# Unscaled first blocks at three norms, a norm of the input by chunks, and modulation blocks summed earlier

## The chip, the cores and the metric

The kernel runs on one core of one Trainium2 chip. The metric is the device time of one launch in microseconds (us). Three runs of the kernel before took 2051.9, 2055.06 and 2056.86 us; the median is 2055.06 us.

## The reference

Two transformer blocks are applied to a sequence of 512 tokens of 1024 features, all in float32. Cut to the parts that matter here:

```
mod = silu(c) @ w_mod[l] + b_mod[l]          # 6 vectors of 1024 for each of 2 layers
sh1, sc1, g1, sh2, sc2, g2 = split(mod, 6)
u  = rms_norm(h,  norm1_g) * (1 + sc1) + sh1      # layer 0: tokens x
uc = rms_norm(ctx, norm1_g) * (1 + csc1) + csh1   # layer 0: 256 context tokens, own c_ctx
f, q, k, v = split(u @ w_in); kc, vc = split(uc @ w_in[:, 1024:])
q, k, kc = rms_norm over each head of 64
y = concat(fourier_mix(f), neighbourhood_attention(q, k, v, kc, vc)) @ w_out
h = h + g1 * y
h = h + g2 * (relu(modulate(rms_norm(h, norm2_g), sh2, sc2) @ w1) ** 2) @ w2
# layer 1: the same with a pooling mixer in place of the attention
# second block:
h = h + merged(rmsnorm(h, norm_mix_g) @ w_in_2 ...) @ w_out_2
u = rmsnorm(h, norm_ffn_g)
h = h + (silu(u @ w_gate) * (u @ w_up)) @ w_down
return rmsnorm(h, norm_final_g)
```

A root-mean-square norm divides each token by one number and multiplies each feature by a gain. So `(g * h / r) @ w` equals `((g * h) @ w) / r`: the division by `r`, one number for each token, may stand behind the product. A shift `s` that is added before the product adds `s @ w`, one number for each output feature.

## The kernel before, in words

All activations lie transposed in SBUF: 8 chunks (KC) of 128 features by 512 tokens. `h` is the residual. A product takes its input as a high and a low part, `uh`/`ul` or `ah`/`al`. Its weights come in blocks of 1024 by 256 (1 MB). SyncE (SP) loads block b into one of four `raw` buffers, ScalarE (ACT) rounds it to `wh` (`split`, L495), GpSimd (POOL) subtracts to get `wl` in four instructions (L880), and TensorE (PE) runs three passes for each chunk and each half of the block (L982 to L984): 48 matmuls of 512 columns. There are two buffers of `wh`/`wl` and four PSUM banks for products, two to a block, so block b needs the buffers and the banks of block b-2 back. Nothing but this fixed order and the semaphores sets the schedule: each engine has its program written out by hand, and every semaphore wait stands in that program.

**Norms** (`norm_sum`, L1028 on; `norm`, L1460 on). ACT squares the chunks of `h`, POOL adds them up, PE sums over the partitions with matmuls of one column (L1041, L1044), ACT takes the root (L511), DVE the reciprocal (L1457), PE spreads it over the partitions (L1050), and DVE and ACT build chunk by chunk: DVE scales (L1467), ACT rounds (`highs`, L523 or L525), DVE subtracts (L1474 or L1472). Small matmuls (`keep_clock`, L1026) are put between. The products behind the norm begin as chunks arrive. The names of the norms are x and ctx (opening), mlp0, pool, mlp1, mix2, ffn and final.

**Opening.** The vectors sh1 and sc1 for x and for ctx come from 8 weight blocks `modf`. PE multiplies them by the two columns of `csil` as stationary operand (L1072), giving 2 rows by 2048; DVE copies the rows, and PE turns them into columns (L1077). Then the norm of x is built, then blocks 0 and 1 (v, by token), the norm of ctx, and the context's v (from L982 with `uch`). Blocks 2 to 7 (k, q, f) follow; beside them run ten head norms (`HN`): PE sums (L1084), ACT root (L551 or L553), DVE reciprocal and product (L1533, L1536), in the places that `HN_AFTER` lists. Block 4 needs the banks that head norms 0 and 1 free.

**Modulation.** The other modulation vectors come from 40 blocks `w_modr`, in the order m = 0, 1, 2, ... DVE sums a block in four instructions (`mod_sum`, L1498 and L1501), PE turns two blocks' sum into columns (`mod_columns`, L1061: four fp32 matmuls of one column, shown as eight instructions), DVE stores them (`mod_store`, L1511). Blocks 0 to 3 stand in the opening, 4 to 11 (`MOD_EARLY` to `MOD_MID`) in the Fourier stage, 12 to 15 beside w_out, 16 on in the first MLP. SP loads block m after block m-2 is summed, in its one queue, in program order with the weights and with 32 small copies `vwin`.

## Time and profile before

| | before |
|---|---|
| median of 3 runs | 2055.06 us |
| profiled execution, its own time | 2056.09 us |
| span of the profile | 2054.2 us |
| PE busy (matmul) | 2002.2 us, 97% |
| DVE, ACT, POOL busy | 930.8, 667.1, 920.0 us |
| mean granted TensorE clock | 0.987 of full |

The profiled execution's own time is 1.9 us above its span; the span is what the engines' rows cover. PE busy is the share of time with a matmul in flight, not the share of peak.

### The profile page before, as it was taken

What the parts mean: (1) busy time and instruction counts of PE and PEld (TensorE: products, weight loads), DVE (VectorE), ACT (ScalarE), POOL (GpSimd) and SP (SyncE); (2) the same over time, 40 slices, a digit from 0 to 9 for tenths busy, and PEclk for the clock granted to TensorE, in tenths of its full rate; (3) what the DMA queues carried; (4) which work ended last, traced back from release to release, by engine and by line L of the source; (5) the groups of instructions that cost most, each with busy time, mean ns of one, the idle gap of its engine ahead of it and who ended that gap; (6) DMA issues with size and microseconds to landing.
All of it is one profiled execution on the core that took longest, in us unless ns stands there. A gap on an engine that the chain in (4) does not pass through costs nothing. (4 is left out here: it accounts for less than half of the span.)

```text
span 2054.2 us, 25743 instructions
## 1 busy us (share of the span) xinstructions
PE 2002.2 (97%) x10096; PEld 1633.8 (80%) x10096; DVE 930.8 (45%) x1422; ACT 667.1 (32%) x872; POOL 920.0 (45%) x704
## 2 busy tenths in 40 slices
PE   7998899999999999999999999999999999999998
PEld 3886578888888888888888866888888878888887
DVE  0546885755748352323233265266664433223123
ACT  2322553222212332212223355356554232222122
POOL 2333345545555535445445312543444455444445
PEclk9899999999999989999999999999999999999999
DMA  8144341625334222222222202222222222222221
GB/s 350 57 143 150 131 152 75 246 91 194 147 153 175 84 83 92 102 102 83 101 102 89 82 22 78 82 83 83 72 73 82 103 82 89 96 102 100 85 82 42
DMA packets 42629, 222.92 MB, mean 109 GB/s; under 512 B 12721, under 2 KB 13233, under 8 KB 17329
## 3 DMA queue, kind: packets, MB, share of 16 engines
q1 hardware_dynamic: 42544, 221.77, 30.0%
q8 instruction: 57, 0.93, 0.2%
q14 instruction: 28, 0.22, 0.0%
HBM read 217.55 MB, written 2.10 MB: 107 GB/s over the span
## 5 line engine op out<-in xcount | busy, mean ns | idle before, releaser
L880 POOL TENSOR_TENSOR wl<-raw,wh 128x512 fp32r<-128x512 f32 x611 | 836.4, 1400 | 1010.9 <-ACT wh L495 911.7
L982 PE MATMUL bank<-uh,wh 128*128 128x512 f32 x1480 | 590.8, 399 | 2.2 <-DVE ul L1472 0.5
L984 PE MATMUL bank<-uh,wl 128*128 128x512 f32 x1480 | 576.9, 390 | 0.0
L983 PE MATMUL bank<-ul,wh 128*128 128x512 f32 x1480 | 576.7, 390 | 0.0
L495 ACT ACTIVATE wh<-raw 128x2048 fp32r<-128x2048 f32 (+1 forms) x149 | 281.3, 1888 | 589.6 <-PE bank L984 586.8
L982 PEld LDWEIGHTS bank<-uh,wh 128*128 128x128 f32 x1480 | 277.8, 188 | 76.8 <-issue 11.1
L984 PEld LDWEIGHTS bank<-uh,wl 128*128 128x128 f32 x1480 | 277.8, 188 | 59.2
L983 PEld LDWEIGHTS bank<-ul,wh 128*128 128x128 f32 x1480 | 278.0, 188 | 58.1 <-issue 3.6
L982 PE MATMUL bank<-ah,wh 128*128 128x512 f32 x816 | 321.3, 394 | 0.0
L984 PE MATMUL bank<-ah,wl 128*128 128x512 f32 x816 | 320.3, 393 | 0.0
L983 PE MATMUL bank<-al,wh 128*128 128x512 f32 x816 | 317.5, 389 | 0.0
L984 PEld LDWEIGHTS bank<-ah,wl 128*128 128x128 f32 x816 | 153.2, 188 | 34.7
L983 PEld LDWEIGHTS bank<-al,wh 128*128 128x128 f32 x816 | 153.2, 188 | 34.3
L982 PEld LDWEIGHTS bank<-ah,wh 128*128 128x128 f32 x816 | 153.4, 188 | 31.3 <-issue 0.2
L1611 DVE SCALAR_TENSOR_TENSOR h<-bank,modc,h 128x512 f32<-128x512 f32 x72 | 53.3, 750 | 268.1 <-PE bank L984 268.1
L1501 DVE SCALAR_TENSOR_TENSOR acc<-mraw,csil,acc 128x512 f32<-128x512 f32 x112 | 141.0, 1259 | 3.7
L638 ACT ACTIVATE r<-bank 128x512 f32<-128x512 f32 x64 | 38.3, 598 | 249.4 <-PE bank L984 248.8
L1641 DVE TENSOR_TENSOR v<-r 128x512 f32<-128x512 f32 x64 | 51.6, 807 | 115.7 <-ACT r L638 115.7
L982 PE MATMUL bank<-wh,uh 128*128 128x256 f32 (+1 forms) x256 | 76.3, 298 | 8.9 <-DVE ul L1474 7.3
L1609 DVE TENSOR_TENSOR h<-bank,h 128x512 f32<-128x512 f32 x32 | 22.1, 692 | 136.7 <-PE bank L984 136.7
L983 PE MATMUL bank<-wl,uh 128*128 128x256 f32 (+1 forms) x256 | 74.1, 290 | 0.0
L984 PE MATMUL bank<-wh,ul 128*128 128x256 f32 (+1 forms) x256 | 74.0, 289 | 0.0
(228 smaller groups left out, 1982.5 us busy)
## 6 DMA issues: line engine op xcount, KB each, us to landing
raw<-in_w SPq DMA_DIRECT2D x64, 1024.0 KB, 5.5
mraw<-in_w_modr SPq DMA_DIRECT2D x32, 1024.0 KB, 4.9
raw<-in_w_gu SPq DMA_DIRECT2D x22, 1024.0 KB, 4.9
raw<-in_w_hg SPq DMA_DIRECT2D x16, 1024.0 KB, 5.0
modf<-in_w_modf SPq DMA_DIRECT2D x8, 1024.0 KB, 17.9
raw<-in_w_in SPq DMA_DIRECT2D x8, 1024.0 KB, 16.7
raw<-in_w_out SPq DMA_DIRECT2D x8, 1024.0 KB, 6.0
mmid<-in_w_modr SPq DMA_DIRECT2D x8, 1024.0 KB, 4.9
```

The costliest lines, as they stand in the source:

```text
L495: act.activation(wh[:, b % 2, 0:nk], raw[:, s, 0:nk], ACT.Copy).then_inc(split_hi, 1)
L638: act.activation(r1[:, m % 2], bank[bi][:], ACT.Relu).then_inc(bank_free[bi], 1)
L880: last = pool.tensor_tensor(wl[:, b % 2, k:k + 2], raw[:, b % RAW, k:k + 2], f32(wh[:, b % 2, k:k + 2]), ALU.subtract)
L982: pe.matmul(out, ah_, bh, start=first, stop=False)
L983: pe.matmul(out, ah_, bl, start=False, stop=False)
L984: return pe.matmul(out, al_, bh, start=False, stop=last)
L1501: dve.scalar_tensor_tensor(a, part[:, k], csil[:, k0 + k, 0:1], a, ALU.mult, ALU.add).then_inc(macc, 1)
L1609: ins = dve.tensor_tensor(h[:, m, :], bank[bi][:], h[:, m, :], ALU.add)
L1611: ins = dve.scalar_tensor_tensor(h[:, m, :], bank[bi][:], gate, h[:, m, :], ALU.mult, ALU.add)
L1641: dve.tensor_tensor(v1[:, m % 2], r1[:, m % 2], r1[:, m % 2], ALU.mult).then_inc(square_ready, 1)
```

## The change

1. *Opening by chunks.* The `modf` blocks are reordered so that block u holds shift and scale of chunk u. `csil` is padded to 32 columns (`csilp`), and the 8 chunks of a block go to four groups of 32 output partitions (`first_rows`). ACT copies 128 by 256, and two matmuls with `sel` add the four partial sums into columns (`first_columns`). DVE makes the gain (`columns_ready`), scales, and subtracts for this chunk, and PE multiplies blocks 0 and 1 by that chunk (`chunk_products`). x is loaded in two halves ahead of the `modf` blocks, its squares are added by DVE, those of ctx by POOL. 30 `keep_clock` matmuls begin the program.
2. *Unscaled first blocks.* At mlp0, mix2 and ffn (`EARLY`) ACT and DVE also make a high and low part of `h` times the gain, without the division (`plain_highs`, `plain_lows`). The first block takes these (`first_product`), with the norm's sum put before its chunk 2 and the spread before its chunk 4. DVE copies the spread factors (`rsb`) and, when the norm is done, multiplies the first block's two banks by them into `tt` (`first_scale`); ACT goes on from `tt`. For mlp0 the shift's part is 16 fp32 matmuls of one column on the raw weights (`shift_columns`), added as a bias.
3. *Modulation.* `MOD_EARLY` goes from 4 to 8: blocks 4 to 7 are summed before the first head norm.
4. The ffn's loop of two and the first group of mlp0 are written out.

```diff
-MOD_EARLY, MOD_MID = 4, 12
+EARLY = {"mlp0": 0, "mix2": 1, "ffn": 2}
+MOD_EARLY, MOD_MID = 8, 12
 # SP, opening
-            sp.dma_start(modf[:, 0], t["w_modf"][0]).then_inc(modf_in[0], 16)
-            sp.dma_start(h[:], t["xT"]).then_inc(x_in, 16)
-            for i in range(1, 8):
-                if i == 6:
-                    load(0, t["w_in"][0])
+            for i in range(2):
+                sp.dma_start(h[:, 4 * i:4 * i + 4, :], t["xT"][:, 4 * i:4 * i + 4, :]).then_inc(x_in[i], 16)
+            load(0, t["w_in"][0])
+            for i in range(8):
                 sp.dma_start(modf[:, i], t["w_modf"][i]).then_inc(modf_in[i], 16)
+                if i == 3:
+                    load(1, t["w_in"][1])
+                if i == 5:
+                    sp.dma_start(ctxT[:], t["ctxT"]).then_inc(ctx_in, 16)
...
             for b in range(8):
                 if 4 <= b + 2 <= 8:
                     load(b + 2, t["w_in"][b + 2] if b < 6 else t["w_out"][0])
-                if b < MOD_EARLY:
-                    load_mod(b)
+                if 2 * b < MOD_EARLY:
+                    load_mod(2 * b)
+                    load_mod(2 * b + 1)
 # ACT
-            squares("mlp0", h, (6, 7))
+            statistics("mlp0", (6,))
+            split(FIRST["mlp0"] + 1)
+            statistics("mlp0", (7,))
             root("mlp0")
-            highs("mlp0", lambda k: mod(0, 3, k), uh, beside=FIRST["mlp0"] + 1)
+            highs("mlp0", lambda k: mod(0, 3, k), uh)
...
+                            if first and j == 0:
+                                act.wait_ge(bank_free[bi], used(b0) + 1)
+                                act.wait_ge(ccol_ready, 1)
+                                act.wait_ge(square_ready, SQ0 + 32 * layer + m - 1)
+                                act.activation(r1[:, m % 2], tt[:, half], ACT.Relu, bias=ccol[:, half:half + 1]).then_inc(first_done, 1)
+                                continue
 # PE
+            def first_product(name, b):
+                def ready(k):
+                    if k == 2:
+                        norm_sum(name)
+                    if k == 4:
+                        norm_spread(name)
+                    pe.wait_ge(xlo_ready, 8 * EARLY[name] + k + 1)
+                product(b, *plain(name), ready=ready)
+            def first_rows(u):
+                pe.wait_ge(modf_in[u], 16)
+                if u >= 2:
+                    pe.wait_ge(mod0_ready, u - 1)
+                for k in range(KC):
+                    g = k % 4
+                    last = pe.matmul(bank[4 + u % 2][32 * g:32 * g + 32, 0:2 * P], csilp[:, k, :], modf[:, u, k, :], start=(k < 4), stop=(k >= 4))
+                last.then_inc(rows_full, 1)
+            for u in (2, 3, 4):
+                first_rows(u)
+                chunk_products(0, u - 2)
+                first_columns(u)
+            chunk_products(0, 3)
+            first_rows(5)
+            first_columns(5)
+            chunk_products(0, 4)
+            first_rows(6)
+            chunk_products(0, 5)
+            first_columns(6)
...
+            MOD_AT = {(2, 0): 1, (3, -1): 2, (4, 0): 3}
...
-                mod_columns(MOD_EARLY // 2 + g)
+                if g < 2:
+                    mod_columns(MOD_EARLY // 2 + g)
+            def shift_columns(b):
+                pe.wait_ge(raw_full[b % RAW], 16 * (b // RAW + 1))
+                for half in range(2):
+                    for k in range(KC):
+                        last = pe.matmul(bank[4][:, half:half + 1], raw[:, b % RAW, k, P * half:P * half + P], mod(0, 3, k), start=(k == 0), stop=(k == KC - 1))
+                last.then_inc(ccol_full, 1)
 # DVE
+                if name == "x":
+                    for k in range(KC):
+                        scaled(k)
+                        low(k)
+                        if k < KC - 1:
+                            columns_ready(k + 1)
+                    return
...
+            def first_scale(name, b):
+                for half in range(2):
+                    bi = bank_of(b, half)
+                    dve.wait_ge(bank_full[bi], used(b) + 1)
+                    if half == 0:
+                        dve.wait_ge(rsb_ready, EARLY[name] + 1)
+                        dve.wait_ge(ulo_ready, 8 * NORM[name] + 8)
+                    dve.tensor_tensor(tt[:, half], bank[bi][:], rsb[:], ALU.mult).then_inc(bank_free[bi], 1)
```

The change moves instructions at three places that matter below. The first is PE at the start of the program, before the change; `modf`/`csil` are the modulation rows, `con` is the identity or the ones, `wh`/`uh` the first product.

```order
L1072 MATMUL bank<-modf,csil 2x256 x32
L1041 MATMUL bank<-con,sqs_94 128x1 x4
L1044 MATMUL bank<-con,sq 128x1 x4
L1050 MATMUL bank<-con,rc 128x128 x4
L1072 MATMUL bank<-modf,csil 2x256 x32
L1077 MATMUL bank<-con,modrow 128x2 x16
L982 MATMUL bank<-wh,uh 128x256
```

The same engine and place after the change.

```order
L1121 MATMUL bank<-con 128x128 x30
L1185 MATMUL bank<-con,sqx 128x1 x4
L1201 MATMUL bank<-modf,csilp 32x256 x8
L1147 MATMUL bank<-con,rc 128x128 x4
L1208 MATMUL bank<-con,modrow 128x2 x2
L1201 MATMUL bank<-modf,csilp 32x256 x8
L1208 MATMUL bank<-con,modrow 128x2 x2
L1201 MATMUL bank<-modf,csilp 32x256 x8
L1221 MATMUL bank<-wh,uh 128x256
```

The first product begins after three of eight row groups instead of after all of them. The second place is DVE between the norm of ctx and the first head norms, before; `acc` is a modulation sum, `RECIPROCAL tt` the start of a head norm.

```order
L1498 TENSOR_SCALAR acc<-mraw,csil 128x512
L1501 SCALAR_TENSOR_TENSOR acc<-mraw,csil,acc 128x512 x7
L1511 TENSOR_TENSOR modc<-bank,bmod 128x4
L1498 TENSOR_SCALAR acc<-mraw,csil 128x512
L1501 SCALAR_TENSOR_TENSOR acc<-mraw,csil,acc 128x512 x3
L1533 RECIPROCAL tt<-tt 128x512
L1536 SCALAR_TENSOR_TENSOR kT<-bank,vec,tt 128x512
```

After:

```order
L1727 TENSOR_SCALAR acc<-mraw,csil 128x512
L1730 SCALAR_TENSOR_TENSOR acc<-mraw,csil,acc 128x512 x7
L1727 TENSOR_SCALAR acc<-mraw,csil 128x512
L1730 SCALAR_TENSOR_TENSOR acc<-mraw,csil,acc 128x512 x7
L1740 TENSOR_TENSOR modc<-bank,bmod 128x4
L1727 TENSOR_SCALAR acc<-mraw,csil 128x512
L1730 SCALAR_TENSOR_TENSOR acc<-mraw,csil,acc 128x512 x7
L1740 TENSOR_TENSOR modc<-bank,bmod 128x4
L1727 TENSOR_SCALAR acc<-mraw,csil 128x512
L1730 SCALAR_TENSOR_TENSOR acc<-mraw,csil,acc 128x512 x7
L1740 TENSOR_TENSOR modc<-bank,bmod 128x4
L1762 RECIPROCAL tt<-tt 128x512
```

Twelve instructions on three blocks have become 32 on eight, all ahead of the first head norm. The third place is ACT around the norm mlp0, before; `uh<-tt` are the high parts behind the norm, `wh<-raw` a weight split (L493 and L484 are the halves of block 13), `r` the ReLU of a finished block.

```order
L506 ACTIVATE sq<-h 128x512 [waits sq_added,bank_free3]
L511 ACT_TABLE_LOAD
L511 ACTIVATE rc<-bank,con 128x4 [waits sum_full]
L525 ACTIVATE uh<-tt,modc 128x512 [waits t_ready] x2
L493 ACTIVATE wh<-raw 128x1024 [waits bank_full3,raw_full1]
L525 ACTIVATE uh<-tt,modc 128x512 [waits t_ready]
L484 ACTIVATE wh<-raw 128x1024
L525 ACTIVATE uh<-tt,modc 128x512 [waits t_ready] x5
```

After:

```order
L529 ACTIVATE wh<-raw 128x2048 [waits bank_full3,raw_full1]
L540 ACTIVATE sq<-h 128x512 [waits sq_added,bank_free3]
L548 ACTIVATE ah<-h,gm 128x512 [waits bank_free3]
L560 ACT_TABLE_LOAD
L560 ACTIVATE rc<-bank,con 128x4 [waits sum_full]
L574 ACTIVATE uh<-tt,modc 128x512 [waits t_ready] x8
L711 ACTIVATE r_107<-tt,ccol 128x512 [waits square_ready,ccol_ready,bank_free0]
L711 ACTIVATE r_107<-tt,ccol 128x512 [waits square_ready,ccol_ready,bank_free1]
L529 ACTIVATE wh<-raw 128x2048 [waits bank_full1,raw_full2]
```

The split of block 13 has moved ahead of the last square. The split of block 14 (the last row) stands behind two ReLUs that read `tt`, which DVE writes after the whole norm; they used to read the banks of block 12 (`r<-bank`).

## Rows read from the trace of the kernel before

**Rows 1.** Who PE waited for: total us, times, longest us.
```profile
PE bank L1061 <- DVE modc L1511: 5.6, 2, 3.5
PE bank L1061 <- DVE acc L1501: 4.8, 1, 4.8
```
**Rows 2.** Timeline of PE, opening: start us, us, line, out<-in, count [idle before].
```profile
9.85 6.39 PE L1072 MATMUL bank<-modf,csil 128*2 128x256 f32 x16 [9.85 <-DMA modf<-in_w_modf]
17.12 10.52 PE L1072 MATMUL bank<-modf,csil 128*2 128x256 f32 x48 [0.88 <-DMA modf<-in_w_modf]
...
45.15 3.73 PE L1077 MATMUL bank<-con,modrow 2*128 2x2 f32 x32
...
86.41 0.28 PE L982 MATMUL bank<-wh,uch 128*128 128x256 f32 x1
...
134.83 0.80 PE L982 MATMUL bank<-uh,wh 128*128 128x512 f32 x1
```
**Rows 3.** Timeline of ACT and DVE, opening.
```profile
29.71 1.90 ACT L495 ACTIVATE wh<-raw 128x2048 fp32r<-128x2048 f32 x1
...
51.14 0.75 DVE L1474 SCALAR_TENSOR_TENSOR ul<-tt,modc,uh 128x512 fp32r<-128x512 f32 x1
...
75.11 0.87 DVE L1467 SCALAR_TENSOR_TENSOR tt<-ctxT,gm,bank 128x256 f32<-128x256 f32 x2 [0.80 <-PE bank L1050]
...
82.31 0.48 DVE L1474 SCALAR_TENSOR_TENSOR ucl<-tt,modx,uch 128x256 fp32r<-128x256 f32 x1 [0.18 <-ACT uch L525]
```
**Rows 4.** Timeline of DVE and SP, 82 to 127 us.
```profile
83.23 5.54 DVE L1501 SCALAR_TENSOR_TENSOR acc<-mraw,csil,acc 128x512 f32<-128x512 f32 x7
...
99.67 4.16 DVE L1501 SCALAR_TENSOR_TENSOR acc<-mraw,csil,acc 128x512 f32<-128x512 f32 x3
...
123.50 3.35 DVE L1533 RECIPROCAL tt<-tt 128x512 f32<-128x512 f32 x1 [19.68 <-ACT tt L553]
...
95.81 20.98 SPq L405 DMA_DIRECT2D vwin<-vnat  x32
```
**Rows 5.** DMA issues of the page: count, KB each, median us to landing.
```profile
mraw<-in_w_modr SPq DMA_DIRECT2D x32, 1024.0 KB, 4.9
```
**Rows 6.** Timeline of PE at the norms mlp0, mix2 and ffn.
```profile
327.00 0.95 PE L1061 MATMUL bank<-con,acc 128*128 128x1 f32 x8
...
358.61 1.05 PE L1061 MATMUL bank<-con,acc 128*128 128x1 f32 x8
...
1097.46 0.40 PE L984 MATMUL bank<-ah,wl 128*128 128x512 f32 x1
...
1128.59 0.39 PE L982 MATMUL bank<-uh,wh 128*128 128x512 f32 x1
...
1672.65 0.39 PE L984 MATMUL bank<-uh,wl 128*128 128x512 f32 x1
...
1676.28 1.16 PE L1050 MATMUL bank<-con,rc 128*128 128x128 f32 x8 [0.18 <-DVE rc L1457]
...
1702.98 0.39 PE L982 MATMUL bank<-uh,wh 128*128 128x512 f32 x1
```
**Rows 7.** Timeline of DVE and POOL at the norms mlp0 and mix2.
```profile
350.29 6.14 POOL L880 TENSOR_TENSOR wl<-raw,wh 128x512 fp32r<-128x512 f32 x4 [6.22 <-ACT wh L495]
...
1103.09 1.40 DVE L1467 SCALAR_TENSOR_TENSOR tt<-h,vec,bank 128x512 f32<-128x512 f32 x2 [2.17 <-PE bank L1050]
...
1113.80 1.60 DVE L1472 TENSOR_TENSOR ul<-tt,uh 128x512 fp32r<-128x512 f32 x2
...
1120.48 5.04 POOL L880 TENSOR_TENSOR wl<-raw,wh 128x512 fp32r<-128x512 f32 x4 [6.22 <-ACT wh L495]
1131.36 5.04 POOL L880 TENSOR_TENSOR wl<-raw,wh 128x512 fp32r<-128x512 f32 x4 [5.84 <-ACT wh L495]
```
**Rows 8.** Busy us (count) of each engine in the Fourier stage, granted clock, DMA.
```profile
191.00:228.00 37.00, 26.43 (x103) 15.59 (x104) 28.60 (x40) 5.73 (x9) 12.04 (x14) 0.90 0.73 267
```
**Rows 9.** Timeline of PE in the attention: matmuls that alternate between two halves.
```profile
235.32 0.66 PE L1206 MATMUL bank<-pT,vwin 128*64 128x128 f32 x8
```

More of the change, by code:

```diff
@@ L1623, in _, with group @@
                     mod_store(MOD_MID // 2 + (b - 8) // 2)
+            plain_lows("mlp0", (6, 7))
             dve.wait_ge(mcol_used, MOD0 // 2)
-            gain_of(2, modc[:, 32:40], vec[:, V_G2:V_G2 + 8])
             def mlp(layer):
                 b0, n0 = FIRST[f"mlp{layer}"], 32 * layer
-                with dve.Fori(0, 4) as q:
+                def group(q, last=False, first=False):
                     for j in range(8):
+                        if first and j == 0:
+                            first_scale("mlp0", b0)
                         if layer == 0 and j < 6:
@@ L1639, in mlp @@
                             dve.wait_ge(bank_free[bi], used(b0 + j, q, 8) + 1)
+                            if first and j == 0:
+                                dve.wait_ge(first_done, 2 * EARLY["mlp0"] + half + 1)
                             dve.wait_ge(a_lo, SQ0 + n0 + m - 1 + 8 * q)
@@ L1988, in layout @@
     con[:, C_ONV:C_ONV + P] = 1 / P
+    for e in range(2):
+        con[e::32, C_SEL + e] = 1
     t["consts"] = con
```

389 lines of the change are left out of this document (271 added, 118 removed).

## The prediction

> **What bounds the kernel now.** I read the page first (PE busy 97% of the span), so only time in which PE waits, or works on something that isn't a product, can be won. The list of PE's waits came next [rows 1]: the reader is to see that it is short, and that its middle lies in the Fourier stage, where PE waits for modulation sums (4.8 us once, 5.6 us in two waits, the longer 3.5). Then I read PE's timeline at four places. In the opening [rows 2], row matmuls run until 45.15 us and the first ctx product starts at 86.41; between them PE works off blocks 0 and 1. At the three norms [rows 6] the reader is to take two instants each: the end of the last product ahead of the norm, and the start of block 2 behind it (of the column sums behind block 1 for mlp0). They lie 358.61 - 327.00 = 31.6, 1128.59 - 1097.69 = 30.9 and 1702.98 - 1672.88 = 30.1 us apart (the products' starts plus 0.23). A block of 48 matmuls takes 10.9 us, which is also the distance of two splits of a POOL that keeps pace [rows 7], so each norm costs 8 to 10 us over two blocks. That is what part 2 aims at. All sums go against the profiled execution's own 2056.09 us; the median is 1.0 lower.
>
> **The opening, until the first ctx product.** A megabyte lands each 2.42 us: the first `modf` at 9.85, and three more (2 of h, 1 of `modf`) by 17.12 [rows 2]. In the new order `modf` 0 is the fourth megabyte, at 17.1; 2 and 3 follow at 22.0 and 24.4, 6 and 7 (behind raw 1 and ctx) at 36.5 and 38.9. The sum of squares is ready by then, since ACT and DVE keep up with h, and the 30 small matmuls run before it, in time in which PE waits anyway.
>
> A row group of 8 matmuls of 256 columns now uses 32 output partitions. No row shows four groups. The nearest shows two halves in turn: 8 instructions of 128 columns in 0.66 us [rows 9], where 8 of the same length on the whole array take 1.16 [rows 6], a factor of 1.75. The old group took 10.52 / 3 = 3.5 us [rows 2]. Bounds: 3.5 (no overlap) and, with the factor applied twice, 1.14. I take 1.1, because alternation did overlap in the one place where it is used. The Trainium skill ("TensorEngine Tiling (Array Packing)", Theoretical Speedup) gives up to 4x at 32 or less, which would make it 0.9; the same page (Key Properties) speaks against the change, since a switch of tiling mode drains the engine, and here it switches twice a chunk. No row here prices the drain. By the one or the other the sum stays, as DVE paces this loop.
>
> For each chunk DVE scales (0.75), ACT rounds (about 0.7), DVE subtracts (0.75) [rows 3], and then DVE makes the next gain in two small instructions (0.5, estimated): 2.7 us in series, where before two chunks overlapped. PE needs 1.1 (rows) + 12 x 0.12 (products) + 0.5 (columns) = 3.0. First chunk: 17.1 + 1.1 + 1.2 (spread) + 1.2 (copy and columns) + 0.5 + 2.2 = about 23. Seven more at 2.7: 42. To that come a weight split on ACT of 1.9 [rows 3], the squares of ctx (1.4), and columns 6, which stand on PE behind a product of a chunk not ready before (2.1): 47. Then sum, root and spread of ctx behind further products (4), and the norm of ctx, 82.79 - 75.11 = 7.7 [rows 3]: 59. I add 2 for POOL beside DVE and for a clock that may be half (16 instructions at 0.40 us each instead of 0.22 in [rows 2] show what it does). First ctx product at 61 instead of 86.41: **-25.4**. Bounds: 57.5 (-29) and, with rows at 2 us, 65 (-21.4).
>
> **Modulation ahead of the head norms.** Block 4 needs the bank that head norm 0 frees. Before, it began 48.4 us after the ctx product [rows 2]. Now two more column sums (0.95 each) lie between, so PE is there at 61 + 48.4 + 1.9 = 111.3. DVE starts its eight sums at 61. Seven instructions take 5.54 us (0.79 each) alone and three take 4.16 (1.39) beside POOL [rows 4]; a block landing takes 4.9 [rows 5], and each load waits for the sum two before it. So: blocks 0, 1 until 67; 2 from 68.8 until 74.3; 3 until 78.5; 4, 5 until 87.5. SP then issues 32 `vwin` copies, 20.98 us [rows 4], with weight block 5 and modulation blocks 6 and 7 queued behind: 6 lands at 106, 7 at 108.5, summed at 112.5. Head norm 0 (3.35 and 0.75) ends at 116.7. Before, DVE stood idle for 19.68 us there, which is the cover that is now used up. Wait of PE at block 4: **+5.4** (bounds 0 and 12), column sums **+1.9**. Later head norms take 4.1 to 4.5 each against 6.4 of PE, so DVE catches up.
>
> In the Fourier stage two of four column sums go, with their waits: 5.6 (both on `mod_store`, [rows 1]) and 2 x 1.05. **-7.7**. The 4.8 us wait stays: its loads are still held until block 7 is done. Bounds: -9 and -4 (if attention then waits for its mask).
>
> **The unscaled first blocks.** Let t = 0 be the end of the last product. PE runs chunks 0 and 1 (2.7), the sum (two groups like the 0.95 of [rows 6]: 2.0), chunks 2 and 3 (7.5), the spread (1.16: 8.7), the rest: block 0 is done at 14.0 and block 1, whose chunks come in time, at 24.9. That alone would win 5 to 6 us for each norm. But the DVE norm starts at 8.8. It takes 1115.40 - 1103.09 = 12.3 us [rows 7], of which POOL's split beside it made 1.2; that split has moved ahead, but a copy of 0.7 is added: it ends at 20.6. At mix2 ACT's table load and sigmoid for `lbs` come next (0.7). Then `first_scale` twice 0.7: 22.7. Then ACT writes twice from `tt` (23.5), and only then splits block 2 (1.9: 25.4), and POOL subtracts four times: 5.04 us, or 6.14 with DVE summing beside it [rows 7]. Block 2's weights are ready at 30.7. PE waits 5.9 us.
> - mix2: 30.7 against 30.9: **-0.1**.
> - ffn: no `lbs`, but the sigmoid's table load of 1.3 stands behind `first_scale`: 31.1 against 30.1: **+1.0**.
> - mlp0: all 1.0 later for the column sum, subtraction of 0.75, POOL at 6.14: 32.4 against 31.6, **+0.8**; and `shift_columns`, 16 matmuls where 4 take 0.95: 3.8 to 4.2, with nothing to hide them: **+4.0**.
>
> Behind each wait, and behind the one at block 4, I expect the clock to fall. In the Fourier stage, with a wait of 4.8 us in it, the mean granted clock is 0.90 over 37 us [rows 8]: 7.4 us at half. Some of that lies in the wait; I take 2.5 us lost for each of four: **+10** (bounds 0 and 14).
>
> **Sum.** -25.4 + 5.4 + 1.9 - 7.7 - 0.1 + 1.0 + 4.8 + 10 = -10.1. 2056.09 - 10.1 = 2046.0, against the median: **2045**.
>
> **Rivals.**
> - *Unscaled blocks work as they read* (ACT's split isn't late). For it: SP, raw buffers and banks are free early. Against: the order of ACT. Block 2 then starts at 24.9 (25.9 at mlp0): PE wins 6.0 at mix2, 5.2 at ffn and 31.6 - 25.9 - 4.0 = 1.7 at mlp0, and only block 4's clock loss stays: -25.4 + 5.4 + 1.9 + 2.5 - 7.7 - 12.9 = -36.2: **2019**. Chance 0.09.
> - *The waits come but the clock holds*: -20.1: **2035**. For it: the other short waits of rows 1 did no visible harm. Chance 0.22.
> - *The modulation chain is longer*: `vwin` waits for copies behind ctx, POOL slows DVE, head norm 0 ends 6 us later, and the Fourier gain is 4: **2053** at most, same or just faster. Chance 0.12.
> - *Slower: row groups don't overlap.* Then PE paces the opening at 3.5 us a group, not DVE: 8 x 2.4 more, less 1 us of slack for each chunk: ctx starts some 13 us later, and at half clock (0.40 an instruction) for part of them 20 later. **2058 to 2065**, taken 2063. It decides from about 2.3 us a group on: there the -10.1 is used up. For it: the two-half row is half evidence, and products of full width stand between groups. Chance 0.09.
>
> **How the numbers follow.** My forecast (waits behind `first_scale`, clock falls) has 0.48, with 2038 to 2051 as its own range. Against a median of 2055.06 a difference of 0.2% is 4.1 us. Faster by more than that: all of the first two rivals, 0.45 of the forecast's 0.48, half of the third: 0.82. Within: 0.08. Slower: 0.10. Range: the first rival and the tail of the last are left out: 2029 to 2054.
>
> **What would show it.** In the profile after: the first ctx product near 61 us and rows in groups of about 1.1 us; DVE's first reciprocal of a head norm near 112 and a PE wait of some 5 us before block 4; one Fourier wait for `acc` and none for `modc`; behind each unscaled block 1 a PE wait of about 6 us for POOL's `wl`, with a lowered clock behind it; 32 instructions of `shift_columns` in 4 us. Wrong if PE's waits for `wl` stay under 2 us at the norms, if the rows take over 2 us, or if the ctx product starts later than 66.

## The result, and the profile after

The changed kernel is slower. Its median is 2062.64 us (2059.7 to 2067.26, 8 runs) against 2054.71 (2051.9 to 2057.68, 8 runs) for the kernel before: a ratio of 1.004, 95% interval [1.0031, 1.005]. The forecast was 2045, in a range of 2029 to 2054; some +8 us came where -10 was expected. The profiled execution took 2061.93 us (span 2060.1, mean granted clock 0.983; before 0.987).

PE's timeline at the places that the prediction named (columns as in [rows 2]); L1201 are the row groups, L1398 `shift_columns`, L1077 and its two neighbours the products, which were L982 to L984:

```profile
16.66 1.07 PE L1201 MATMUL bank<-modf,csilp 128*32 128x256 f32 x16
...
60.67 0.39 PE L1077 MATMUL bank<-wh,uch 128*128 128x256 f32 x1 [0.59 <-DVE ucl L1677]
...
75.31 0.39 PE L1077 MATMUL bank<-uch,wh 128*128 128x256 f32 x1 [2.20 <-POOL wl L971]
...
113.85 1.02 PE L1231 MATMUL bank<-sq,con 128*128 128x512 f32 x2
122.69 0.77 PE L1077 MATMUL bank<-uh,wh 128*128 128x512 f32 x1 [7.83 <-DVE kT L1765]
123.26 0.63 PE L1078 MATMUL bank<-ul,wh 128*128 128x512 f32 x1
...
299.85 4.74 PE L1398 MATMUL bank<-modc,raw 128*128 128x1 f32 x32
304.46 0.77 PE L1077 MATMUL bank<-uh,wh 128*128 128x512 f32 x1
...
349.81 0.79 PE L1077 MATMUL bank<-uh,wh 128*128 128x512 f32 x1 [6.48 <-POOL wl L971]
...
1124.85 0.79 PE L1077 MATMUL bank<-uh,wh 128*128 128x512 f32 x1 [5.14 <-POOL wl L971]
1125.44 0.63 PE L1078 MATMUL bank<-ul,wh 128*128 128x512 f32 x1
...
1705.45 0.79 PE L1077 MATMUL bank<-uh,wh 128*128 128x512 f32 x1 [5.50 <-POOL wl L971]
```

The reader is to see that nearly everything the prediction named is there: rows in 1.07 us, the first ctx product at 60.67 instead of 86.41, a wait at block 4, and three waits for `wl` of 5.1 to 6.5 us at the norms. Behind the waits at block 4 and at the norms, and behind the column sums, the granted clock stands at 0.50: there the second and the following products last 0.63 us where they last 0.39 elsewhere. (A first product of 0.77 or 0.79 us alone doesn't show it; run 6 has one of 0.79 at a granted clock of 1.00.) So the total isn't explained by looking where the change was made. What finds the rest is the start of the same product in both kernels. Both have 7848 product matmuls; I numbered them in order of time and took the difference after minus before at ten of them.

| up to (number of the product) | before, us | after, us | difference | change over the stretch | predicted for it |
|---|---|---|---|---|---|
| first ctx product (192) | 86.41 | 60.67 | -25.74 | -25.7 | -25.4 |
| first of block 4 (480) | 134.83 | 122.69 | -12.14 | +13.6 | +7.3 |
| first of block 6 (576) | 161.09 | 151.13 | -9.96 | +2.2 | +2.5 |
| first of `w_out` (672) | 282.45 | 266.13 | -16.32 | -6.4 | -7.7 |
| block 4 of mlp0 (1056) | 382.22 | 374.31 | -7.91 | +8.4 | +7.3 |
| end of mlp1 (4000) | 1090.36 | 1087.34 | -3.02 | **+4.9** | **0** |
| behind mix2's block 2 (4200) | 1144.91 | 1142.85 | -2.06 | +1.0 | +2.4 |
| ahead of the ffn's norm (6000) | 1612.83 | 1614.72 | +1.89 | **+4.0** | **0** |
| behind ffn's block 2 (6500) | 1734.71 | 1738.69 | +3.98 | +2.1 | +3.5 |
| last (7847) | 2041.35 | 2047.53 | +6.18 | **+2.2** | **0** |

The predicted terms add up to -10.1, the measured ones to +6.2. Of the 16.3 us between them, 11.1 lie in three stretches that the change does not touch (bold), and 6.3 between the first ctx product and block 4. The table compares one profile with one profile. The fifteen profiles here that have the new opening put the first ctx product between 58.53 and 62.33 us, so that entry is good to some 2 us.

**The plain products.** A plain product is one with no norm or head norm beside it. In the second layer's MLP, blocks that read the activations `ah` and `al` run as 192 matmuls without anything between. The first and last of such a run, in the kernel before and after (PE's timeline):

```profile
791.12 0.40 PE L982 MATMUL bank<-ah,wh 128*128 128x512 f32 x1
...
834.86 0.39 PE L984 MATMUL bank<-ah,wl 128*128 128x512 f32 x1
```

```profile
785.04 0.40 PE L1077 MATMUL bank<-ah,wh 128*128 128x512 f32 x1
...
829.60 0.39 PE L1079 MATMUL bank<-ah,wl 128*128 128x512 f32 x1
```

191 intervals take 43.74 us before and 44.56 after: 229.0 and 233.3 ns, start to start, while the busy time of one is 0.39 to 0.40 in both. Products that read `uh` and `ul` come every 226.7 ns in both kernels. The clock is at its upper level (1.00) over both of these runs of 192. The page before counts 816 matmuls of each of three kinds on `ah` and `al` (2448 x 4.33 ns = 10.6 us); the page after counts 848, since the unscaled first blocks read `ah` too.

The three stretches are not explained by this alone, though the sums look alike. The intervals on `ah` and `al` in them grew by 5.5, 1.4 and 2.3 us, 9.1 of the 11.1 (the first stretch gave 0.6 back elsewhere). In the middle one, from mix2's block 2 to the ffn's norm, 2.6 more go with the clock: the profile after has two stretches of 3.4 us at half there (from 1165.7 and 1268.1 us), the one before has none. The code of this stretch doesn't fix them. With the region where the changed kernel has it, the stretch takes 469.0 to 469.2 us in the profiles without half clock (runs 1, 5 and 9 below), 470.3 to 470.5 with one such stretch (7, 8, 10) and 471.7 to 471.9 with two (6 and the changed kernel); before it took 467.9. What starts them stays open. So only 1.2 to 1.4 of the 4.0 us belong to the pace of `ah`.

What differs for `ah` and not for `uh` is its address. The change replaced

```
modx = at("modx", [P, 16], F32, o); o += 64
mx = at("mx", [P, KC, 2, 2], F32, o); o += 128
```

and all tiles of the region behind the weights (`A`), `ah` and `al` among them, moved up by 64 bytes per partition: the region's address was 134848, which is 192 modulo 256, and is now 134912, 0 modulo 256.

**The wait at block 4.** DVE and SP's queue, same views as [rows 4]:

```profile
89.45 0.15 DVE L1740 TENSOR_TENSOR modc<-bank,bmod 128x4 f32<-128x4 f32 x1
111.48 0.49 DVE L1727 TENSOR_SCALAR acc<-mraw,csil 128x512 f32<-128x512 f32 x1 [21.87 <-DMA mraw<-in_w_modr]
112.00 6.42 DVE L1730 SCALAR_TENSOR_TENSOR acc<-mraw,csil,acc 128x512 f32<-128x512 f32 x7
118.35 0.15 DVE L1740 TENSOR_TENSOR modc<-bank,bmod 128x4 f32<-128x4 f32 x1
118.42 3.33 DVE L1762 RECIPROCAL tt<-tt 128x512 f32<-128x512 f32 x1
...
81.41 20.88 SPq L437 DMA_DIRECT2D vwin<-vnat  x32
102.40 0.53 SPq L399 DMA_DIRECT2D raw<-in_w_in  x1
102.97 0.93 SPq L408 DMA_DIRECT2D mraw<-in_w_modr  x2
```

DVE stands still for 21.87 us until modulation block 6 is there, because its load is issued behind the 32 copies. That is the predicted chain; but the block's data is there at 111.5, not at 106, so the reciprocal begins at 118.42 instead of 112.5. The copies are issued nearly when they were forecast to be; the load behind them then takes 8.5 us to land where [rows 5] have 4.9, with a weight load issued just ahead of it and the DMA engines busy for 0.99 of the last 4.5 us. The granted clock behind it (windows; columns as in [rows 8]):

```profile
122.80:127.90 5.10, 5.10 (x12) 3.99 (x13) 5.07 (x3) 1.02 (x2) 0.00 (x0) 0.50 0.60 92
```

PE itself was ready for block 4 at 114.9 (122.69 less the wait of 7.83), 3.6 us later than the 111.3 of the prediction: at block 2 it had waited 2.20 us for `wl`, with the clock at half for 3.4 us behind it. In this kernel that costs nothing, because the wait at block 4 swallows it; where that wait is gone (runs 6 and 14) it counts.

**The norm of mlp0.** DVE, ACT and POOL behind the norm:

```profile
339.25 1.29 DVE L1710 TENSOR_TENSOR tt<-bank,rsb 128x512 f32<-128x512 f32 x2
...
339.97 1.34 ACT L711 ACTIVATE r<-tt,ccol 128x512 f32<-128x512 f32 x2 [1.64 <-DVE tt L1710]
341.22 1.90 ACT L529 ACTIVATE wh<-raw 128x2048 fp32r<-128x2048 f32 x1
...
343.20 6.55 POOL L971 TENSOR_TENSOR wl<-raw,wh 128x512 fp32r<-128x512 f32 x4 [17.93 <-ACT wh L529]
```

ACT's split of block 2 does stand behind `first_scale`'s readers, and PE waits until POOL has subtracted. Who PE waited for, in all:

```profile
PE bank L1077 <- POOL wl L971: 21.2, 6, 6.5
PE bank L1077 <- DVE kT L1765: 7.8, 1, 7.8
...
PE bank L1176 <- DVE acc L1730: 4.8, 1, 4.8
```

Beside [rows 1]: the waits for `modc` are down from 5.6 to 0.2, `acc` stayed, and 29.0 us for `wl` and `kT` have come, of which the kernel before had 2.6 (for `wl`). Against that stand the products' waits for `ul`, 7.8 before and 2.3 after.

### The profile page after: what moved, and what is told of

Read it like the earlier page. It is cut to its first block and busy times, and to the rows that moved or that the text cites. A ratio compares the mean times of both kernels' runs of the same rounds, so it can differ in the third digit from the quotient of the medians.

```text
span 2060.1 us, 25693 instructions
## 1 busy us (share of the span) xinstructions
PE 1993.8 (97%) x10116; PEld 1633.1 (79%) x10116; DVE 965.4 (47%) x1471; ACT 683.0 (33%) x900; POOL 916.3 (44%) x699
## 5 line engine op out<-in xcount | busy, mean ns | idle before, releaser
L1077 PE MATMUL bank<-uh,wh 128*128 128x512 f32 x1432 | 574.8, 401 | 26.0 <-POOL wl L971 17.4
L1079 PE MATMUL bank<-uh,wl 128*128 128x512 f32 x1432 | 561.9, 392 | 0.0
L1078 PE MATMUL bank<-ul,wh 128*128 128x512 f32 x1432 | 561.7, 392 | 0.0
L1077 PEld LDWEIGHTS bank<-uh,wh 128*128 128x128 f32 x1432 | 271.4, 190 | 95.7 <-POOL wl L971 27.7
L1077 PE MATMUL bank<-ah,wh 128*128 128x512 f32 x848 | 336.3, 397 | 0.0
L1079 PE MATMUL bank<-ah,wl 128*128 128x512 f32 x848 | 334.8, 395 | 0.0
L1078 PE MATMUL bank<-al,wh 128*128 128x512 f32 x848 | 334.8, 395 | 0.0
L1077 PEld LDWEIGHTS bank<-ah,wh 128*128 128x128 f32 x848 | 159.5, 188 | 37.9 <-issue 0.3
L1730 DVE SCALAR_TENSOR_TENSOR acc<-mraw,csil,acc 128x512 f32<-128x512 f32 x126 | 150.3, 1193 | 6.1 <-DMA mraw<-in_w_modr 1.7
L1886 DVE TENSOR_TENSOR al<-v,ah 128x512 fp32r<-128x512 f32 x64 | 59.0, 923 | 2.2
L1077 PE MATMUL bank<-wh,uh 128*128 128x256 f32 (+1 forms) x192 | 54.9, 286 | 2.7 <-POOL wl L971 1.6
L2148 DVE TENSOR_TENSOR gz<-bank,gs 128x512 f32<-128x512 f32 x20 | 13.8, 692 | 93.0 <-ACT gs L949 93.0
## 6 DMA issues: line engine op xcount, KB each, us to landing
raw<-in_w_in SPq DMA_DIRECT2D x8, 1024.0 KB, 13.3
```

Of the source, the lines that this page charges most:

```text
L1077: pe.matmul(out, ah_, bh, start=first, stop=False)
L1078: pe.matmul(out, ah_, bl, start=False, stop=False)
L1079: return pe.matmul(out, al_, bh, start=False, stop=last)
L1730: dve.scalar_tensor_tensor(a, part[:, k], csil[:, k0 + k, 0:1], a, ALU.mult, ALU.add).then_inc(macc, 1)
L1886: dve.tensor_tensor(al[:, m], v1[:, m % 2], f32(ah[:, m]), ALU.subtract).then_inc(a_lo, 1)
```

## The experiments

Theory A (the region's place costs 11 us), B (the order on SP makes head norm 0 late), C (ACT's order at the three norms and the column sums eat what the early start brings). The rival to each is that the loss belongs to something else of the change, and would stay. Ratios are to the kernel before, run beside each on the same chip. Differences to the changed kernel are differences of medians from different sets of runs, in which the median of the kernel before lay between 2054.71 and 2055.86, and are good to 2 or 3 us.

### The place of the activations

**1. The kernel before, region moved by 64 bytes.**
```diff
-        modx = at("modx", [P, 16], F32, o); o += 64
+        modx = at("modx", [P, 16], F32, o); o += 128
```


> The kernel before, with one edit: the tile ahead of the activations' region is given 128 bytes of room instead of 64, so the region (ah, al and all that is laid over them) starts 64 bytes further on in each partition, as it does in the changed kernel. No instruction changes. Theory (address): in the changed kernel the matmuls that read ah or al follow each other at 233.3 ns instead of 228.9 in the first MLP's twin of layer 1, with the same code; the 64 bytes cause it. 816 x 3 such matmuls x 4.4 ns: slower by about 10.8 us (8 to 13), and the interval is 233 ns in the trace. Rival (another chip or run, or an edit elsewhere that loads SBUF): no difference from before beyond 2 us, interval 229 ns.

Measured: 2065.67 us, ratio 1.005 [1.0037, 1.0063], some +10 us. The run of 192:

```profile
791.30 0.40 PE L982 MATMUL bank<-ah,wh 128*128 128x512 f32 x1
...
835.86 0.39 PE L984 MATMUL bank<-ah,wl 128*128 128x512 f32 x1
```

233.3 ns each. Sixty-four unused bytes make the kernel before at least as slow as the changed one, without any of its work. Theory A stands.

**2 and 3. The changed kernel, region moved by 192 and by 128 bytes more.**
```diff
-        A = (o + 31) // 32 * 32
+        A = (o + 31) // 32 * 32 + 192      # run 3: + 128
```


> The changed kernel, with the activations' region moved by 192 bytes, so that it lies 256 bytes behind where it lies in the kernel before. Theory (address, with a period of 256 bytes or less): the ah and al matmuls come at 228.9 ns again, 848 x 3 x 4.4 ns = 11.2 us less than the changed kernel: about 2051, 3 to 4 us faster than before. Rival (not the address): unchanged at about 2062.

> The changed kernel, with the region moved by 128 bytes. uh, ul, wh and wl all start at 128 past a multiple of 256, and uh products come at 226.7 ns; now ah and al start at 128 past a multiple of 256 too. Theory (the offset within 256 bytes decides): ah and al matmuls at 226.7 ns, 848 x 3 x 6.6 ns = 16.8 us less than the changed kernel: about 2046. Theory (it is the distance in bytes from the engines' other reads, not the offset): anything from 2046 to 2062. Rival (not the address): 2062.

Measured: by 192 (the place of before, 192 modulo 256) 2051.51 us, 0.9986 [0.9976, 0.9997], interval 229.0 ns; by 128 2048.02 us, 0.996 [0.9945, 0.9975], 226.7 ns, as for `uh`, which also stands at 128 modulo 256. The change alone, in the place of before, is faster than before by 3 us (0.5 to 5), not slower.

**4. The kernel before, region moved by 192 bytes.**
```diff
-        A = (o + 31) // 32 * 32
+        A = (o + 31) // 32 * 32 + 192
```


> The kernel before with the region behind the weights moved up by 192 bytes per partition and nothing else; with it the activations' high and low parts stand at 128 modulo 256, as the input's parts do. Address theory: the products that read them come every 226.7 ns instead of 228.98 ns, as they did in the changed kernel moved by 128 bytes; 2448 products times 2.3 ns give -5.6 us against before: some 2049 us. Rival (what the moved versions gained was of the changed kernel, not of the address): no change, 2055 us.

Measured: 2051.21 us, 0.998 [0.997, 0.999], and the run of 192:

```profile
785.29 0.39 PE L982 MATMUL bank<-ah,wh 128*128 128x512 f32 x1
...
828.59 0.39 PE L984 MATMUL bank<-ah,wl 128*128 128x512 f32 x1
```

226.7 ns. The interval is as expected; the gain of 3.7 us in the medians is less than 5.6, which lies just inside the ratio's interval (-2.1 to -6.2 us). Three places are known, the fourth multiple of 64 was not tried, and whether the address itself decides or its distance to another tile's stays open.

### The wait at block 4

**5. Blocks 6 and 7 back in the Fourier stage.**
```diff
-MOD_EARLY, MOD_MID = 8, 12
+MOD_EARLY, MOD_MID = 6, 12
...
-            MOD_AT = {(2, 0): 1, (3, -1): 2, (4, 0): 3}
+            MOD_AT = {(2, 0): 1, (3, -1): 2}
...
```


> The changed kernel, but with MOD_EARLY at 6: modulation blocks 6 and 7 go back to the Fourier stage, and no modulation load stands behind the 32 vwin copies and ahead of the head norms. Theory (the wait of PE at block 4, 7.8 us, is DVE waiting for the mraw load that SP issues behind vwin): DVE ends its sums at about 90 instead of 118 us, the wait at block 4 goes, and with it the 10.2 us of halved clock there (some 3.5 lost); the Fourier stage takes back one wait of 2 to 3.5 and a column sum of 1. Together 8 to 9 us faster than the changed kernel, about 2054. Rival (DVE's own sums are the bound, or the Fourier stage takes it all back): within 3 us of the changed kernel.

Measured: 2049.32 us, 0.9981 [0.9971, 0.9992], 13.3 us below the changed kernel. The wait at block 4 is gone, with its half clock; 2.6 us of waits for `modc` came back. That is 4 to 5 us more than my price for it.

**6. The copies behind the loads, all eight blocks early.**
```diff
-                if b == 2:
+                if b == 3:
                     for bi in range(4):
                         sp.wait_ge(bank_free[bi], 1)
                     for w in range(QT):        # the 32 copies into vwin
```


> The changed kernel with SP issuing the 32 copies into vwin behind the loads of modulation blocks 6 and 7 instead of ahead of them. If head norm 0 was late because VectorE's sums of blocks 6 and 7 waited for loads that stood behind these copies (copies issued from 81.4 to 102.3, the loads at 103.0, VectorE idle until 111.5), the 7.8 us wait at block 4 goes and with it the half clock behind it: -13 us as with blocks 6 and 7 back in the Fourier stage, 2049 us. Rival (the head norm is late by VectorE's own work on eight blocks, whenever the loads come): the wait shrinks by less than 2 us, 2060 us.

Measured: 2049.94 us, 0.9972 [0.9962, 0.9983]: -12.7, as theory B said. SP, DVE and PE:

```profile
82.84 5.36 SPq L408 DMA_DIRECT2D mraw<-in_w_modr  x2
88.38 21.73 SPq L437 DMA_DIRECT2D vwin<-vnat  x32
...
94.20 5.83 DVE L1730 SCALAR_TENSOR_TENSOR acc<-mraw,csil,acc 128x512 f32<-128x512 f32 x4 [1.62 <-DMA mraw<-in_w_modr]
99.95 0.15 DVE L1740 TENSOR_TENSOR modc<-bank,bmod 128x4 f32<-128x4 f32 x1
100.03 3.34 DVE L1762 RECIPROCAL tt<-tt 128x512 f32<-128x512 f32 x1
...
111.03 1.02 PE L1231 MATMUL bank<-sq,con 128*128 128x512 f32 x2
111.49 0.79 PE L1077 MATMUL bank<-uh,wh 128*128 128x512 f32 x1
```

The same sums end 18.4 us earlier (99.95 instead of 118.35), and PE goes from the head sum to block 4 without a wait. The copies take as long to issue as before (21.73 us); they now stand behind the loads. DVE's work was not too much; the wait was made by a queue.

### The unscaled first blocks

**7. The split of block 2 ahead of the sixth high part.**
```diff
-            highs("mlp0", lambda k: mod(0, 3, k), uh)
-            highs("mix2", None, uh)
-            highs("ffn", None, uh)
+            highs("mlp0", lambda k: mod(0, 3, k), uh, early=FIRST["mlp0"] + 2)
+            highs("mix2", None, uh, early=FIRST["aq"] + 2)
+            highs("ffn", None, uh, early=FIRST["ffn"] + 2)
 # in highs()
+                    if early is not None and k == 5:
+                        split(early)
...
```


> The changed kernel, with ACT's split of block 2 behind the norms mlp0, mix2 and ffn put ahead of the norm's sixth high part instead of behind the two reads of the scaled banks. Theory (the gain of the unscaled blocks is lost on ACT's order): PE's waits of 6.5, 5.1 and 5.5 us for wl at block 2 go to under 1 us each, with the lowered clock behind them (6.8, 3.4 and 3.4 us at half, worth half of that): 17.1 + 6.8 - 2 = 20 to 24 us faster than the changed kernel, about 2041. Rival (the wait moves on, since first_scale frees the banks at the same instant): under 8 us faster, a wait for tt or bank at block 2 or 3 instead.

Measured: 2044.62 us, 0.9943 [0.9929, 0.9957], 18 us below the changed kernel, a little short of the 20 to 24 expected. The profiled execution was the slowest of its six (2050.76). At mix2 and ffn no wait is left. PE's list:

```profile
PE bank L1081 <- DVE kT L1769: 12.5, 1, 12.5
PE bank L1081 <- POOL wl L975: 8.5, 4, 6.4
```

At mlp0 the wait only moved from block 2 to block 3: SP issues the next weight block behind a modulation load that waits for `mod_sum(16)`, and DVE made that sum only behind `first_scale`. And the wait at block 4 grew to 12.5 in this profile although the product before it came earlier: block 4 starts at 123.71 here and at 122.69 in the changed kernel, whatever PE does before, because the chain of loads sets it.

**8. Fourteen of the sixteen column-sum matmuls left out** (the bias of mlp0's first block is then not the reference's).
```diff
-                    for k in range(KC):
-                        last = pe.matmul(bank[4][:, half:half + 1], raw[:, b % RAW, k, P * half:P * half + P], mod(0, 3, k), start=(k == 0), stop=(k == KC - 1))
+                    last = pe.matmul(bank[4][:, half:half + 1], raw[:, b % RAW, 0, P * half:P * half + P], mod(0, 3, 0), start=True, stop=True)
```


> The changed kernel with 14 of the 16 matmuls of shift_columns left out; only the first chunk of each half is multiplied, so the bias of mlp0's first block is not the reference's. Theory 1 (cost of the matmuls alone): they ran from 300.1 to 304.5 us, so 14 of 16 are worth 3.9 us: about 2058.7. Theory 2 (one-column matmuls count as idle for the clock, since it was halved from 302.1 to 309.0): 3.9 + 2.4 of block 11's 13.3 instead of 10.9: 6.3 us faster, about 2056.

Measured: 2057.21 us, 1.001 [1.0002, 1.0019], 5.4 below the changed kernel. What is left of the sums, and the product behind:

```profile
300.44 0.50 PE L1397 MATMUL bank<-modc,raw 128*128 128x1 f32 x4
300.80 0.49 PE L1077 MATMUL bank<-uh,wh 128*128 128x512 f32 x1
301.12 0.40 PE L1078 MATMUL bank<-ul,wh 128*128 128x512 f32 x1
```

The clock stays up here. In the changed kernel it fell to half at 302.1, while the 32 were still running, and stayed there until 309; the window from their end:

```profile
304.40:309.10 4.70, 4.70 (x12) 3.73 (x13) 0.16 (x1) 0.00 (x0) 4.56 (x5) 0.52 0.00 0
```

From `w_out` to block 0 of mlp0 the difference to before changed by -6.7 us here and by -0.4 in the changed kernel, 6.3 between them: 4.3 from the sums and 2.1 behind them. That is what theory 2 had said for the profiles; the medians (5.4) lie between the two theories (3.9 and 6.3). PE was never idle there, and I had priced a fall of the clock behind waits alone.

**9. PE kept busy ahead of block 2.**
```diff
+                            if first and j == 2:
+                                keep_clock(20)      # likewise ahead of block 2 at mix2 and ffn
```


> The changed kernel with 20 small matmuls (identity by identity, 4.9 us at full clock, their result unused) on PE ahead of block 2 behind mlp0, mix2 and ffn, in the time in which PE waits for wl (6.5, 5.1 and 5.5 us). The waits stay, only PE's clock is kept. Theory (the idle wait lowers the clock, 6.8, 3.4 and 3.4 us at half behind the three waits): 5 to 7 us faster than the changed kernel, about 2056. Rival (the clock falls whatever PE does in the wait, or what is lost there is regained later): within 2 us of 2062.

Measured: 2059.14 us, 1.0022 [1.0013, 1.0031], -3.5. By the product starts mix2 gains 1.5 us and ffn 1.3, block 2 of mlp0 nothing (its clock is still at half from 348.3). In this profile the half clock at the column sums, which this edit does not touch, lasted 3.4 us and not 6.8, which brought 1.6: its length varies from one execution to the next. The clock loss behind the `wl` waits at mix2 and ffn was 1.3 to 1.5 us, not the 2.5 that I took for each. The median gained less than the theory's price of the idle clock, 5 to 7 us, and more than the rival's 2.

**10. The three norms as before**, opening, modulation and region as changed.
```diff
-EARLY = {"mlp0": 0, "mix2": 1, "ffn": 2}
+EARLY = {}
...
-            first_product("mix2", b0)
+            normalise("mix2")
...
```


> The changed kernel with the norms ahead of mlp0, mix2 and ffn as they were before (no shift of the columns, no unscaled blocks); opening, early modulation blocks and the region's place stay as changed. By the product marks the three places cost 9.1, 1.4 and 2.0 us: this theory expects -12.5 us against the changed kernel, 2050 us. Rival: the early start there pays for its half-clocked stretches, so that undoing it brings nothing or a loss: 2062 us or more.

Measured: 2050.1 us, 0.9972 [0.9961, 0.9982]: -12.5, as the product starts had said (that it fits to the tenth is chance; the medians are not that good). As written, part 2 is a loss in all. How it divides is read from single profiles: between the marks of the table, the changed kernel takes 9.3 us more than this one at mlp0, 0.7 at mix2 and 1.8 at ffn.

### What is left of the parts, and better versions

**11. First combination**: region moved by 128, run 7's early splits, and `mod_sum(16)` between the norm's reciprocal and its first scaling.
```diff
+            norm_factor("mlp0")
+            mod_sum(MOD0, 0, 6)
```


> The changed kernel with the region moved by 128 bytes, the early split of block 2, and at mlp0 DVE's sum of modulation block 16 put between the norm's reciprocal and its first scaling, because SP's load of weight block 15 is queued behind a load that waits for this sum (with the early split alone PE waited 6.4 us at block 3 of mlp0). Theory: 14.6 (128 bytes) + 18.0 (early split) + 6.4 and some 2 of clock: 41 us faster than the changed kernel, about 2022. Rival (the wait at block 15 has another cause, or PE then waits for head norm 0 or for the scaled banks): about 2030.

Measured: 2025.34 us, 0.9855 [0.9841, 0.9869], between the theory (2022) and the rival (2030), 37 us below the changed kernel where 41 were expected. The waits for `wl` are down to 4.9 us in four, the longest 1.7.

**12. Second combination**: the first, with run 5's six early blocks.

> The earlier combination (region moved by 128 bytes, splits of block 2 ahead of the sixth high part, mod_sum(16) behind the norm factor) and with it blocks 6 and 7 back in the Fourier stage. If the wait at block 4 (9.1 us there) and the half clock behind it (10.2 us long) are the same loss as in the changed kernel, this brings the same -13 us against the combination: 2012 us. Rival: the Fourier stage takes the waits back (2.6 us of waits for modc and their clock), so that half of it stays: 2019 us.

Measured: 2017.04 us, 0.9811 [0.9794, 0.9828]: -8.3, between the two theories (2012 and 2019) and nearer the rival.

**13. Third combination**: the second, with mlp0's norm as before.
```diff
-EARLY = {"mlp0": 0, "mix2": 1, "ffn": 2}
+EARLY = {"mix2": 0, "ffn": 1}
-                if b == 11:
-                    shift_columns(FIRST["mlp0"])
...
```


> As the combination before it, but with mlp0's norm as in the kernel before: no shift of the columns, blocks 0 and 1 scaled, mod_sum(16) in its old place. If the column sums and the clock behind them cost more than the early start of mlp0 brings, this is 2 to 4 us faster than the combination with it; if the early start pays, it is slower by 2 to 6 us.

Measured: 2012.04 us, 0.9798 [0.9781, 0.9815]. The median is 5 us lower, the profiled span 4.2 (2013.6 and 2009.4); the intervals overlap, so this is likely, not certain. By the product starts 2.2 us of it lie between `w_out` and block 4 of mlp0.

**14. The opening alone**: norms as before, four blocks early, region moved by 192.

> The changed kernel with only the opening by chunks left: norms as before, four modulation blocks early as before, region moved by 192 bytes more (so at 128 modulo 256). The budget theory: before (2054.9) less 25.4 for the first context product, less 5.5 for the region's place: 2024 us. Rival (much of the opening is given back behind it, by weights or modulation blocks that are not ready): 2035 us or more.

This expectation has an error of mine: 192 bytes more put the changed kernel's region where the kernel before has it (192 modulo 256), not at 128, so no 5.5 us were due, and the theory means 2030.5 (the 2055.9 of the kernel before in this set, less 25.4). Measured: 2032.49 us, 0.9888 [0.9873, 0.9903], -23.4. The difference to before is -24.1 at the first ctx product, -21.0 at `w_out` and -24.4 at the end. What the opening gives reaches the end nearly whole.

**15. Third combination with four early blocks**, as before (`MOD_EARLY = 4`).

> The best combination so far (2012 us: region moved by 128, norms of mix2 and ffn with unscaled first blocks and early split, mlp0 as before, six blocks early) with four blocks early as in the kernel before. If the moved blocks are worth what their waits in the Fourier stage take (some 3 us for two blocks), this is 2015 us. Rival (the sums ahead of the head norms cost as much as they save there): 2012 us or less.

Measured: 2015.7 us, 0.9799 [0.9786, 0.9813]: the median is the theory's, but the ratio is that of run 13 (0.9798), so the two blocks between four and six are not shown to be worth anything.

**16. Third combination with eight early blocks** and run 6's order on SP.

> The same combination with eight blocks early and the copies into vwin behind the loads of blocks 6 and 7. If nothing but the order on SP made eight blocks bad, this is the fastest: 2009 to 2012 us, with no wait of over 1 us at block 4. Rival (eight are too many for VectorE ahead of head norm 0): a wait there and some 2018 us.

Measured: 2011.71 us, 0.9785 [0.9772, 0.9798]: the lowest of all, with run 13 beside it, and 44 us below before. No wait is left at block 4. PE's list (without the ones of the first 30 us), and POOL and ACT at mix2's norm:

```profile
PE bank L1174 <- DVE acc L1726: 4.9, 1, 4.9
PE bank L1075 <- POOL wl L969: 3.1, 3, 1.6
```

```profile
1080.83 6.40 POOL L969 TENSOR_TENSOR wl<-raw,wh 128x512 fp32r<-128x512 f32 x4 [9.36 <-ACT wh L527]
...
1087.88 1.34 ACT L767 ACTIVATE aqT<-tt,vec 128x512 f32<-128x512 f32 x2 [2.24 <-DVE tt L1706]
```

POOL has finished block 2's low part (1087.23) when the scaled bank is read; in the changed kernel it began 1.9 us after that read's end (1119.86 and 1117.98). Four, six and eight early blocks give 2015.7, 2012.0 and 2011.7; the first and the last were run in one set (ratios 0.9799 and 0.9785). Part 3 is worth 3 to 4 us once its load order is mended, with intervals that overlap: likely, not shown.

**The budget.** From the opening alone (2032.5): the order on SP +12.7 (run 6), the three norms +12.5 (run 10), the region at 0 instead of 192 modulo 256 +11.1 (run 2), less some 4 for the early blocks. That makes 2064.8; the changed kernel takes 2062.6. The parts, each measured by an edit that takes it out or puts it right, add up to the whole within 2.2 us, which is about what one median can be off. The sum takes it that they don't act on each other, which no run shows part by part.

## Why the prediction was wrong

One term was absent, and that alone turned the sign; one landing was taken too early; the clock was priced at the wrong places.

- **Products between the norms: 0 in the sum, +11.1 measured.** This is the step that failed. I carried the difference found at one norm unchanged to the next. The sum has no term for what a change of the layout does to instructions that it leaves alone, and the one byte count that would have asked for it (64 to 128) is in the new kernel. By runs 1 and 2 the layout costs 10 to 11 us in the whole kernel; in the profile the three stretches hold 9.1 of it, and 2.6 by two drops of the clock that don't come in every execution. It turned a forecast of the right sign into one of the wrong sign: run 2 is faster than before. Even so its 2051.5 is 6 us above the 2045 forecast, which is the next steps' share. Whether the move would cost or save could not be read from the trace of before, though 226.7 and 229.0 ns for the same matmul stood in it.
- **"The opening": right.** -25.4 predicted, -25.7 measured, 61 and 60.67 us; run 14 confirms -23.4 at the end. That it fits to 0.3 us is partly luck: the same opening took from 58.5 to 62.3 us in other profiles. The loop was also not sized right inside: from the first gain to the last it took 3.9 us a chunk, not 2.7 and a few extras, and the 2 us that I had added for POOL and the clock covered it. By my own figures PE (3.0) and not DVE (2.7) paced it, so there was no slack of 1 us, and the 13 us of the slower rival follow from neither. The row groups came at 1.07 us for 1.1 taken (one at 1.71, at half clock), so the slower rival (3.5 us a group) is false, though its range of 2058 to 2065 holds the result; a number hit for another reason is no support. The Trainium skill ("TensorEngine Tiling (Array Packing)", Theoretical Speedup) gives up to 4x at 32 columns: the trace shows 3.5 / 1.07 = 3.3. The same page of the Trainium skill (Key Properties) says that a change of tiling mode drains the engine: beside a group the trace shows no gap of over 0.1 us that such a drain would make.
- **"6 lands at 106, 7 at 108.5": too early.** +5.4 and +1.9 predicted until block 4, +13.6 measured. Block 4 starts when head norm 0 has freed its bank, whatever PE does before, and that was 122.69 and not 116.7: 5.5 us of it are the landing at 111.5, 8.5 us behind its issue on a busy DMA, where I took 4.9. The wait of 2.20 us and the half clock at block 2, which I had not seen, are hidden in the longer wait here (7.83 instead of 5.4); in run 14, without that wait, the stretch from the ctx product to block 4 is 3.0 us longer than in the kernel before. Run 6 shows the mechanism right (the copies ahead of the loads), and what I missed: that one line of order on SP decides the sign of part 3.
- **Clock: right in kind, wrong in place.** I took 2.5 us for each of four waits. Block 4 cost 2.2, mix2 and ffn 1.5 and 1.3 (run 9). But the column sums cost 2.1 more behind them (run 8), where PE never waited, and the clock fell behind block 2 of the opening too, where it cost nothing here.
- **Waits at the norms: right.** 5.9 predicted (6.5 with mlp0's late sum), 5.14 to 6.48 measured. (By its own terms the 30.7 is 25.4 + 5.04 = 30.4; that slip is too small to matter.) *Unscaled blocks work as they read* gave 6.0 and 5.2 us for mix2 and ffn with ACT's split in time; in run 16 the difference to before falls by 6.4 and 5.8 there. ACT's order decides, as the prediction said. At mlp0 it gave +1.7, and runs 12 and 13 rather show a loss.
- **The Fourier stage: -7.7 predicted, -6.4 measured.** The `modc` waits went, but 1.3 and 1.4 us for `ysb` and `ul` took some of their place.

## What to carry to other kernels

When a total doesn't agree with the places that a change touches, number the instructions that both kernels have and subtract their starts: slow drift in untouched stretches shows at once, and here it pointed to 64 bytes of layout. Then add up the intervals that you blame, and read the granted clock over the same stretch, before you call the drift explained: here the count times the interval (10.6) came near the 11.1 of the three stretches, of which they really held 9.1. Before an edit's worth is judged, put its buffers where they were, or pad them to a known good place, so that the edit and the layout are measured apart. A wait that a change adds need not be made by the work moved; it can be made by what its load or its first reader stands behind in a queue: look for a swap of order before taking the work back; here it was worth 13 us on SP and 18 on ACT.

## What the runs showed of the hardware

- The place of a tile in SBUF changes the pace of the matmuls that read it: 226.7, 229.0 or 233.3 ns for 512 columns of fp32r with the region at 128, 192 or 0 modulo 256 bytes per partition, the clock at its upper level in all (runs 1 to 4). Whether the address or the distance to another tile decides is open. The Trainium skill ("TensorE: Matmul & The Clock Gate", Part 1) gives one figure for 512 columns at that clock, 215.7 ns, and none by address; no run here reached it.
- The clock can fall with no idle time of PE: 32 records of one-column fp32 matmuls ran back to back for 4.74 us, the granted clock fell to half 2.2 us into them and stayed there for 6.8 us (3.4 in run 9), with products of 0.63 us instead of 0.39 behind them. Behind 4 of them (0.50 us) it did not fall.
- Half clock comes and goes between executions of the same code: none, one or two stretches of 3.4 us between mix2's block 2 and the ffn's norm, some 1.4 us each.
- Four groups of 32 output columns overlap: 16 matmul records of 256 columns in 1.07 us, where the form before took 3.5 us for 16.
